# Attention scores as full passes over a zero-padded k, and the row maximum taken as a minimum of negated logits

## What is computed

```python
    n_sel = min(MOBA_TOPK, nb - 1)      # 0 here
...
        logits = jnp.einsum('bhtd,bhsd->bhts', qb, kb, preferred_element_type=jnp.float32) * scale
        logits = logits + F[:, :, start:end, None] - F[:, :, None, :end]
        logits = jnp.where(s_pos <= t_pos, logits, -jnp.inf)
        p = jax.nn.softmax(logits, axis=-1)
```

## Time and profile before

| what | us |
|---|---|
| median of 3 runs | 163.12 |
| the three runs | 162.9, 163.12, 168.15 |
| span of the profiled execution | 161.2 |
| TensorE busy | 146.4 (91%) |
| VectorE busy | 124.8 (77%) |
| ScalarE busy | 112.3 (70%) |
| GpSimd busy | 72.0 (45%) |

### The profile page before, as it was taken

The page is one execution under the profiler, slowest core; times in us unless marked ns, Lnnn a source line. Parts: engine busy times, 40 slices in busy tenths (PEclk is TensorE's granted clock), DMA queues, the critical chain, the costliest instruction groups (busy, mean ns, idle before and its releaser), DMA issues.

```text
span 161.2 us, 2896 instructions
## 1 busy us (share of the span) xinstructions
PE 146.4 (91%) x976; PEld 129.1 (80%) x976; DVE 124.8 (77%) x257; ACT 112.3 (70%) x228; POOL 72.0 (45%) x74
## 2 busy tenths in 40 slices
PE   7699999999958999999798999999998989999950
PEld 7267678889948999988687999998988867889850
DVE  0479976589999989685998989898989989340583
ACT  3589549398835874989959898979969696305330
POOL 7205910000960999504608475744719083501130
PEclk9999999999999999999999999999999999999998
DMA  3999376646796895591556455552526090000024
GB/s 56 304 413 355 123 247 217 250 130 242 262 372 205 357 296 193 169 256 69 150 179 185 140 172 159 139 189 64 157 108 195 0 319 10 0 0 0 4 85 175
DMA packets 12044, 27.99 MB, mean 174 GB/s; under 512 B 1272, under 2 KB 5376, under 8 KB 11776
## 3 DMA queue, kind: packets, MB, share of 16 engines
q1 hardware_dynamic: 11728, 26.52, 49.5%
q10 hardware_dynamic: 304, 1.32, 2.3%
HBM read 24.68 MB, written 1.06 MB: 160 GB/s over the span
## 4 chain that ended last, share of the span: by engine, by line
PE 33%; issue 25%; DVE 16%; POOL 12%; ACT 7%; DMA 3%; SPq 1%; POOLq 1%; DVEq 0%; ACTq 0%
PE bank L791 11%; PE bank L932 10%; PE bank L775 5%; POOL probs L302 5%; DVE w_lo L538 4%; DVE h L616 4%; POOL bias L285 3%; DMA raw<-in_w_units 3%; POOL bias L294 2%; ACT w_hi L354 2%; PE bank L805 2%; DVE h_lo L622 1%; PE bank L885 1%; POOL xg_lo L308 1%; ACT gate L469 1%
## 5 line engine op out<-in xcount | busy, mean ns | idle before, releaser
L538 DVE TENSOR_TENSOR w_lo<-raw,w_hi 128x1024 fp32r<-128x1024 f32 x35 | 51.4, 1475 | 3.7 <-ACT w_hi L354 3.4
L354 ACT ACTIVATE w_hi<-raw 128x1024 fp32r<-128x1024 f32 x35 | 36.8, 1057 | 6.9 <-PE bank L775 2.1
L775 PE MATMUL bank<-h_hi,w_hi 128*128 128x256 f32 x128 | 35.9, 280 | 0.0
L775 PE MATMUL bank<-h_lo,w_hi 128*128 128x256 f32 x128 | 35.8, 279 | 0.0
L775 PE MATMUL bank<-h_hi,w_lo 128*128 128x256 f32 x128 | 35.7, 279 | 0.0
L302 POOL TENSOR_TENSOR probs<-probs,row_inv 128x256 f32<-128x256 f32 (+1 forms) x16 | 12.9, 829 | 36.4 <-DVE row_inv L654 36.4
L313 POOL TENSOR_TENSOR wo_lo<-raw_out,wo_hi 128x1024 fp32r<-128x1024 f32 x4 | 17.4, 4350 | 24.6 <-ACT wo_hi L358 24.6
L775 PEld LDWEIGHTS bank<-h_hi,w_hi 128*128 128x128 f32 x128 | 24.2, 189 | 0.5 <-DVE h_lo L622 0.2
L775 PEld LDWEIGHTS bank<-h_lo,w_hi 128*128 128x128 f32 x128 | 24.0, 188 | 0.2
L775 PEld LDWEIGHTS bank<-h_hi,w_lo 128*128 128x128 f32 x128 | 24.2, 189 | 0.0
L775 PE MATMUL bank<-xg_hi,w_hi 128*128 128x256 f32 x64 | 17.9, 280 | 2.5 <-DVE gate L612 2.5
(11 more groups left out here) (127 smaller groups left out, 336.7 us busy)
## 6 DMA issues: line engine op xcount, KB each, us to landing
raw<-in_w_units SPq DMA_DIRECT2D x31, 512.0 KB, 4.1
raw_out<-in_w_out SPq DMA_DIRECT2D x4, 512.0 KB, 4.5
v_pair<-v SPq DMA_DIRECT2D x8, 256.0 KB, 4.3
raw<-in_w_out SPq DMA_DIRECT2D x4, 512.0 KB, 3.5
x_t<-in_xt SPq DMA_DIRECT2D x4, 256.0 KB, 5.5
squares<-decay_rows_scratch ACTq DMA_DIRECT2D x1, 1024.0 KB, 7.8
x_t<-in_x SPq DMA_DIRECT2D x1, 1024.0 KB, 5.2
out<-x_t SPq DMA_DIRECT2D x3, 256.0 KB, 2.1
```

The source lines that it names most:

```text
L354: nc.scalar.activation(w[0][:, s, :], raw[:, s, :], ACT.Copy).then_inc(s_hi, 1)
L538: nc.vector.tensor_tensor(w[1][:, s, :], raw[:, s, :], w[0][:, s, :].bitcast(F32), ALU.subtract).then_inc(s_lo, 1)
L775: last = nc.tensor.matmul(dst, stationary(a, j), moving(b, j), start=n == 1, stop=n == count * len(PASSES))
```

## The change

`q_stack`, `k_twin` and `mx` go. `q_lo` holds the low part of q of both heads, in the rows in which q lies. `k_wide` is a pair of tiles, high and low part of k, each with a copy for head 0 and one for head 1, and zeros in the other head's rows. Each of the three passes now covers both heads at once. The instruction that adds the bias multiplies by -SCALE and takes the minimum, which is the negated, scaled maximum; the exponential then takes scale -1.

```diff
-        q_stack = sb("q_stack", [P, 2, 2, SEQ], F32R)
-        k_twin = sb("k_twin", [P, 2, SEQ], F32R)
-        k_lo = sb("k_lo", [P, 2, SEQ], F32R)
+        q_lo = sb("q_lo", [P, 2, SEQ], F32R)
+        k_wide = [sb(f"k_wide_{n}", [P, 2, SEQ], F32R) for n in PARTS]
...
-            pool.memset(k_lo[:, :, :].bitcast(F32), 0.0).then_inc(s_const, 1)
+            for part in k_wide:
+                pool.memset(part[:, :, :].bitcast(F32), 0.0).then_inc(s_const, 1)
...
             def exps(i):
                 for a in range(2):
-                    act.wait_ge(s_nmax, 2 * i + a + 1)
+                    act.wait_ge(s_logits, 4 * i + 2 * a + 2)
...
-                                             bias=neg_max[:, c:c + 1], scale=SCALE,
+                                             bias=neg_max[:, c:c + 1], scale=-1.0,
...
-            def query_stack(i, b):
-                act.wait_ge(s_qhi, 3 * i + 1)
-                for a, (own, other) in enumerate(head_rows):
-                    nc.scalar.activation(q_stack[own, b, a, :], q_hi[own, b, :], ACT.Copy).then_inc(s_qhi, 1)
...
-                    nc.scalar.activation(k_twin[own, a, :], bank[1][own, 0:SEQ], ACT.Copy).then_inc(s_khi, 1)
-
-            def key_twin(i):
-                act.wait_ge(s_khi, 2 * i + 2)
-                for a, (own, other) in enumerate(head_rows):
-                    nc.scalar.activation(k_twin[other, a, :], k_twin[own, a, :].bitcast(F32),
-                                         ACT.Copy).then_inc(s_ktwin, 1)
+                for a, own in enumerate(head_rows):
+                    nc.scalar.activation(k_wide[0][own, a, :], bank[1][own, 0:SEQ], ACT.Copy).then_inc(s_khi, 1)
...
                     nc.vector.tensor_tensor_reduce(out=logits[:, a, lo:hi], in0=ps[:, a, :], in1=bias[:, a, lo:hi],
-                                                   scale=1.0, scalar=-3.0e38, op0=ALU.add, op1=ALU.max,
-                                                   accum_out=mx[:, c:c + 1]).then_inc(s_logits, 1)
-                dve.wait_ge(s_logits, 4 * i + 2 * a + 2)
-                nc.vector.tensor_scalar(neg_max[:, 2 * a:2 * a + 2], mx[:, 2 * a:2 * a + 2], -SCALE, None,
-                                        ALU.mult).then_inc(s_nmax, 1)
+                                                   scale=-SCALE, scalar=3.0e38, op0=ALU.add, op1=ALU.min,
+                                                   accum_out=neg_max[:, c:c + 1]).then_inc(s_logits, 1)
...
             def query_low(i, b):
-                dve.wait_ge(s_qhi, 3 * i + 1)
-                for a, (own, other) in enumerate(head_rows):
-                    nc.vector.tensor_tensor(q_stack[other, b, a, :], bank[0][own, 0:SEQ], q_hi[own, b, :].bitcast(F32),
-                                            ALU.subtract).then_inc(s_qlo, 1)
+                dve.wait_ge(s_qhi, i + 1)
+                nc.vector.tensor_tensor(q_lo[:, b, :], bank[0][:, 0:SEQ], q_hi[:, b, :].bitcast(F32),
+                                        ALU.subtract).then_inc(s_qlo, 1)
...
             def scores(i, b):
-                pe.wait_ge(s_qhi, 3 * i + 3)
-                pe.wait_ge(s_qlo, 2 * i + 2)
-                pe.wait_ge(s_ktwin, 2 * i + 2)
+                pe.wait_ge(s_qhi, i + 1)
+                pe.wait_ge(s_qlo, i + 1)
+                pe.wait_ge(s_khi, 2 * i + 2)
                 pe.wait_ge(s_klo, 2 * i + 2)
                 for dst, rows, keys in ((s0_ps, slice(0, P), P), (s1_ps, slice(P, SEQ), SEQ)):
-                    nc.tensor.matmul(dst, q_hi[:, b, rows], k_lo[:, :, 0:keys], start=True, stop=False)
-                    for a in range(2):
-                        last = nc.tensor.matmul(dst[:, a, :], q_stack[:, b, a, rows], k_twin[:, a, 0:keys],
-                                                start=False, stop=a == 1)
+                    nc.tensor.matmul(dst, q_hi[:, b, rows], k_wide[0][:, :, 0:keys], start=True, stop=False)
+                    nc.tensor.matmul(dst, q_hi[:, b, rows], k_wide[1][:, :, 0:keys], start=False, stop=False)
+                    last = nc.tensor.matmul(dst, q_lo[:, b, rows], k_wide[0][:, :, 0:keys], start=False, stop=True)
```

More of the change, by code:

```diff
@@ L48 @@
 WARM_UP = 8
-N_CONST = 3
+N_CONST = 4
 PASSES = ((0, 0), (0, 1), (1, 0))
@@ L103, in hybrid_layer @@
         newton = sb("newton", [P, 2, TT])
-        mx = sb("mx", [P, 4])
         neg_max = sb("neg_max", [P, 4])
@@ L134, in hybrid_layer @@
                       (1, slice(HALF + SEQ, D_MODEL), bank[3][:, 0:SEQ])]
-        head_rows = [(slice(0, HEAD_DIM), slice(HEAD_DIM, P)), (slice(HEAD_DIM, P), slice(0, HEAD_DIM))]
+        head_rows = [slice(0, HEAD_DIM), slice(HEAD_DIM, P)]
         s_g_in, s_wf_in, s_fb_in = sem("g_pre_in"), sem("w_f_in"), sem("f_bias_in")
@@ L165, in hybrid_layer @@
         s_khi, s_klo = sem("k_hi"), sem("k_lo")
-        s_ktwin = sem("k_twin_ready")
         s_qk = sem("scores_ready")
@@ L169, in hybrid_layer @@
         s_logits = sem("logits_ready")
-        s_nmax = sem("neg_max_ready")
         s_exp = sem("exp_done")
@@ L475, in attend @@
                 unit_high((2 * b + 2) % RING, n, 2 * i + QK_0 - 1)
-                if first != 1:
-                    key_twin(i - 1)
                 if first == 0 and not fresh:
@@ L484, in attend @@
                     probs_high(i - 2)
-                query_stack(i, b)
                 if first != 2:
@@ L504, in _ @@
             unit_high(2, 16 * (UNITS // RING + 1), UNITS - 1)
-            key_twin(PAIRS - 1)
             y_high(PAIRS - 3)
@@ L656, in query_low @@
             def query_low(i, b):
-                dve.wait_ge(s_qhi, 3 * i + 1)
-                for a, (own, other) in enumerate(head_rows):
-                    nc.vector.tensor_tensor(q_stack[other, b, a, :], bank[0][own, 0:SEQ], q_hi[own, b, :].bitcast(F32),
-                                            ALU.subtract).then_inc(s_qlo, 1)
+                dve.wait_ge(s_qhi, i + 1)
+                nc.vector.tensor_tensor(q_lo[:, b, :], bank[0][:, 0:SEQ], q_hi[:, b, :].bitcast(F32),
+                                        ALU.subtract).then_inc(s_qlo, 1)
             def key_low(i):
                 dve.wait_ge(s_khi, 2 * i + 2)
-                for a, (own, other) in enumerate(head_rows):
-                    nc.vector.tensor_tensor(k_lo[own, a, :], bank[1][own, 0:SEQ], k_twin[own, a, :].bitcast(F32),
-                                            ALU.subtract).then_inc(s_klo, 1)
+                for a, own in enumerate(head_rows):
+                    nc.vector.tensor_tensor(k_wide[1][own, a, :], bank[1][own, 0:SEQ],
+                                            k_wide[0][own, a, :].bitcast(F32), ALU.subtract).then_inc(s_klo, 1)
             def gated(i):
@@ L901, in _ @@
             key(0, 0)
-            pe.wait_ge(s_qlo, 2)
+            pe.wait_ge(s_qlo, 1)
             query(1, 1)
@@ L907, in attend @@
             def attend(i, b, loads, first=False):
-                pe.wait_ge(s_qlo, 2 * i)
+                pe.wait_ge(s_qlo, i)
                 query(i, b)
```

## The result

Timed on the same chip, the changed kernel takes 0.9697 of the time of before, with a 95% interval of 0.9657 to 0.9737: the medians are 158.55 us against 163.33. By the ratio that is 4.9 us less (4.3 to 5.6), where 3.6 were forecast. The direction and the mechanism were right, and the gain was sized too small; 0.9697 of 163.12 is 158.2, just under the range of 158.4 to 161.8.

A forecast was written before the change was run, and what follows sets the result against it. The loop through VectorE and ScalarE was taken to bound late rounds (9.18 us), level with TensorE in middle ones. Idle time 4.8, less columns 2.0, plus pace 0.8, gives 3.6 off 163.12: 159.5 us, range 158.4 to 161.8.

The forecast's parts named there:

- the idle time: TensorE's gaps in the rounds over head pairs: 5.9 us in all, of which 4.8 would go.
- the units' pace: Projection units behind a gap take 2.83 us, in a stream 2.73; about 8 become quick, 0.8 us gained.
- The columns: Score passes on TensorE: 2304 columns a pair instead of 1536, +0.25 us each, 2.0 over eight pairs.
- The bound and the loop: Late rounds: the loop through VectorE and ScalarE bounds at 9.18 us, falls to 8.54; then TensorE bounds nearly every round.
- VectorE's savings: In VectorE's loop: exponentials start 0.19 us earlier, and one instruction for q's low part saves 0.45.
- TensorE needs 8.4 + 0.25: TensorE's work in a late round: about 8.65 us, or 8.45 with quicker projection units.
- The opening: Rounds of pairs 0 and 1: about 1.2 us gained, copies worth about 0.5 at the first scores.
- The tail: Behind the rounds: the last scores' added columns cost 0.25 us there.
- Off the path: Rival: the rounds' idle time stays and only added columns count, 165.1 us; chance 0.05.
- the second collision: Rival: each round's second VectorE weight unit also meets GpSimd, loop 9.35 us, total 165.7; chance 0.04.
- the dear passes: Rival: score passes cost their recorded lengths, block 2.43 us, total 169.8; chance 0.03.
- the half gain: Rival: the rounds' idle time shrinks only by half, round 8.75 us, total 161.6; chance 0.18.

The follow-up runs named there:

- e10: Changed kernel with the low part of q again in two 64-row instructions and the old row maximum: 162.47 and 163.14 us.
- e7: Kernel before with the two instructions of the second group's bias swapped, the long one first: 161.61 us, ratio 0.989.
- e4: Changed kernel with one more 512-column pass per pair, overwritten by the next pass: 160.15 and 160.26 us, ratio 0.980.
- e6: Changed kernel with the two instructions of the second group's bias swapped, the long one first: 158.61 us, from one execution.
- e1: Kernel before with only the row maximum taken as a minimum, scores and copies as before: 161.97 us, ratio 0.991.
- e8: Kernel before with stacked scores and copies kept, plus the minimum and swapped bias instructions: 159.79 and 160.51 us, ratio 0.980.
- e11: Kernel before with minimum, swapped bias, one instruction for q's low part, its halves moved by GpSimd; stacked scores kept: 159.93 to 162.89 us, ratio 0.984.
- e3: Changed kernel with ScalarE's four copies per pair put back, into a spare tile nobody reads: 158.55 and 158.91 us, ratio 0.971.
- e2: Changed kernel with the old row maximum, its extra instruction and wait: 163.55 to 164.56 us, ratio 1.005, first scores 5 us later.
- e9: Changed kernel with the low part of q again in two instructions of 64 rows: 161.19 and 161.88 us.

## Why the prediction was right, and where it was too small

**The step that failed: the idle time, 4.8 us of the sum.** The sum was 4.8 of idle time gone, less 2.0 for columns, plus 0.8 for the units' pace: 3.6. Idle time was the recorded 3.96 and 12 x 0.16 for what records hide, 5.9 in all. I measured it from start to start instead, from the first q to the last matmul: what each step takes beyond its usual pace (0.116 us for 256 columns, 0.231 for 512, 0.108 for a transpose), where it takes over 0.03 more. That gives some 7.1 us before and 1.2 after, so 5.9 went, and not 4.8. The columns cost 1.9, and the pace gave 0.4 in the units and 0.6 in the transposes: 5.0 in all, as against 4.95 measured from the first q on (94.58 us before, 89.63 after). By place, the idle time that I had missed is in the opening, in the late rounds and behind the last scores, as the next paragraphs say.

**The bound and the loop: right.** VectorE's loop set the late rounds (e10, e7), and after the change TensorE sets them (e4, e6). Six matmuls in 1.14 us, no idle time ahead of the transposes, the collision still there: each was named beforehand.

**The columns: right.** 0.25 a pair was the term. The blocks add up to 8.99 us after and 7.08 before, 1.9 for 2.0.

**VectorE's savings: a little small.** 0.64 per round was forecast and 0.79 came. The single low instruction takes 0.42, but `probs_low` starts 0.35 behind it (111.56 to 111.91), where two took 0.91 up to that start (115.34 to 116.25 before): 0.56 saved, not 0.45. The exponentials gained 0.21, not 0.19.

**The failing step in a late round: "TensorE needs 8.4 + 0.25".** I took TensorE's own work in a round as 9.18 less the two gaps that the rows show. What the middle rounds of e1, e8 and e11 show in its place is 8.07 to 8.11 with the stacked scores. The 0.3 to 0.4 between is nearly all waiting that I had counted as work. Part of it stands in two rows of the kernel before, in the late round from which I argued:

```profile
112.53 0.85 ACT L464 ACTIVATE k_twin<-k_twin 64x256 fp32r<-64x256 f32 x2
...
113.49 0.36 PE L865 MATMUL bank<-k_lo,q_hi 128*128 128x256 f32 x1
```

The copy of k ends at 113.38 and the scores start at 113.49, while the last transpose was under way from 113.31. No idle time is shown there, since the modelled end of the transpose covers it; but from the first transpose to the scores it is 0.78 (112.71 to 113.49), and 0.57 after the change. The rest is one more slow projection unit (0.09) and values that start late (1.12 for 1.05). So a late round came to 8.32, not 8.45, and each gave 0.9 and not 0.7. I also counted four late steps, where the table has three; these two errors cancel, and the late rounds gave 2.7 for 2.8.

**The opening: most of what was missing.** I gave it 1.2 us without adding up its steps, and it gave 2.3 (0.6 + 0.6 + 1.0). The 0.6 ahead of the first scores is from two executions, and holds the wait for the copy of k that e3 does not bring back. e2, e3 and e9 share the two opening rounds out: undoing the maximum costs 0.4 there, the copies 0.5, the two low instructions 1.2, which overlap, since the changed kernel gains 1.6 in those two rounds. I had thought of the opening as ScalarE's alone; VectorE's chain is as tight there. From the start of a pair's scores to that of its exponentials it is 2.88 us before and 2.26 after for pair 0 (69.56 to 72.44, 68.93 to 71.19), and 4.71 and 3.94 for pair 1 (78.29 to 83.00, 77.04 to 80.98). Behind the exponentials come the normalised probabilities, and TensorE's idle times ahead of the values of pair 0 (0.20) and the transposes of pair 1 (0.44) are gone.

**The tail: 0.25 was taken off for the last scores, and nothing was lost.** From the first matmul of the last scores to the last one it is 23.10 us before and 23.13 after. The kernel before waited behind its last scores, for GpSimd's low part of y (line 308):

```profile
132.52 1.73 POOL L308 TENSOR_TENSOR xg_lo<-y,xg_hi 128x256 f32 x1
...
134.03 0.40 PE L932 MATMUL bank<-wo_hi,xg_lo 128*128 128x512 f32 x1
134.40 0.47 PE L932 MATMUL bank<-w_hi,xg_hi 128*128 128x512 f32 x1
134.71 0.40 PE L932 MATMUL bank<-w_lo,xg_hi 128*128 128x512 f32 x1
```

The low part ends at 134.25, and these two steps take 0.37 and 0.31 us where such a step takes 0.23 everywhere around: 0.22 of waiting, and no idle time recorded. In the changed kernel the low part ends at 128.93, TensorE comes to that place at 129.66, and every step there is 0.23. So the wait of 0.22 paid for the 0.25 of columns.

**The units' pace: oversized.** I expected 0.8 us from some 8 units that become quick. Of the 16 units of q and k, 10 were slow before (2.83) and 6 are after, which is 0.4 us. Those of k stayed slow but for one from pair 2 on, though nothing interrupts the stream. So a gap ahead isn't the reason for the slow pace of those, and what is stays open.

**The clearing: nothing, as said.** The first q starts at 60.52 before and at 60.64 after.

**The rivals.** None came about. Off the path is excluded by the recorded idle time of 1.22 us, the second collision by VectorE's loop of 8.39, the dear passes by the block of 1.14, and the half gain by the rounds of 8.32.

## What to carry to other kernels

Where two engines run in loops of nearly the same length, cost a change by the loop in which each edit lies: here 13 us of work off ScalarE gave 0.5 us of the stretch, and 0.8 us a round off VectorE gave nearly all the rest. More work on TensorE cost nothing in rounds that VectorE's loop set (e10: 9.11, 9.23 and 9.17 with the wide passes, 9.18, 9.17 and 9.33 before), and its full price in those that TensorE sets (e4). Take an engine's own work from a round in which it is the bound, not from a slower round less its visible gaps, since modelled matmul ends hide short waits; measure them from start to start. And cost the first rounds by themselves, step by step.

## What was not expected of the hardware

A collision of two engines can hang on little: with GpSimd's bias issued as a short and a long instruction, VectorE's weight unit took 2.04 us; as a long and a short one, 1.46; alone, 1.23. In the changed kernel the long instruction starts at 126.20 and the weight unit at 126.28, 0.08 us too late to be first.

On VectorE the next instruction started 0.35 us after one of 128 rows, before that one's record of 0.42 ended (111.56, 111.91). Two instructions of 64 rows and as many columns took 0.91 us up to the next one's start (115.34 to 116.25).
